# Preparing the linear attention by halves among its chunks, with GpSimd making the differences to the reference columns

## The reference, cut to what matters

```python
cum = jnp.cumsum(gi, axis=2)
diff = cum[:, :, :, None, :] - cum[:, :, None, :, :]
decay = jnp.where(causal, jnp.exp(jnp.where(causal, diff, 0.0)), 0.0)
scores = jnp.einsum('bhid,bhijd,bhjd->bhij', qi, decay, ki)
out = (jnp.einsum('bhij,bhjv->bhiv', scores, vi)
       + jnp.einsum('bhid,bhdv->bhiv', qi * jnp.exp(cum), state))
state = (jnp.exp(last[:, :, 0, :, None]) * state
         + jnp.einsum('bhjd,bhjv->bhdv', ki * jnp.exp(last - cum), vi))
```

## Time and profile before

| | us |
|---|---|
| median of 3 runs (lowest to highest) | 3340.0 (3337.72 to 3342.39) |
| the profiled execution, its time | 3340.4 |
| its span in the trace | 3338.8 |
| `gla_stage`, from its first to its last instruction | 330.2 to 569.8 |
| TensorE busy over the whole span | 2937.0 (88%) |
| VectorE busy over the whole span | 1674.2 (50%) |

### The profile page before, as it was taken

One profiled execution on the slowest core, in us unless ns is written; L12 is line 12 of the kernel. 1 busy time (PEld: TensorE's weight loads), 2 busy tenths in 40 slices (PEclk: granted clock), 3 DMA queues, 4 the chain that ended last, 5 costly groups with the idle time before them and its releaser, 6 DMA issues. The chain is left out here.

```text
span 3338.8 us, 38597 instructions
## 1 busy us (share of the span) xinstructions
PE 2937.0 (88%) x14688; PEld 2323.1 (70%) x14688; DVE 1674.2 (50%) x2776; ACT 979.9 (29%) x1870; POOL 706.7 (21%) x445
## 2 busy tenths in 40 slices
PE   6999456878999999969999799988899998999988
PEld 4767346336888888857768687766677676877766
DVE  4170876223323313232478763476534787634865
ACT  3151221111001001020268342175103673421751
POOL 1233000002333333214111301402141113014021
PEclk8999678888999999989999899999999998999989
DMA  3011001101111121113112001203231120012032
GB/s 106 33 32 38 0 1 50 55 6 67 35 58 51 35 67 45 35 66 105 27 38 76 26 1 51 70 8 126 89 107 26 43 75 23 1 52 73 4 126 89
DMA packets 78797, 168.35 MB, mean 50 GB/s; under 512 B 14848, under 2 KB 33808, under 8 KB 78096
## 3 DMA queue, kind: packets, MB, share of 16 engines
q1 hardware_dynamic: 70160, 140.61, 12.6%
q10 hardware_dynamic: 8448, 25.18, 2.7%
HBM read 128.00 MB, written 20.97 MB: 45 GB/s over the span
## 5 line engine op out<-in xcount | busy, mean ns | idle before, releaser
L296 PE MATMUL psum<-H,ffn_W 128*128 128x512 f32 x672 | 262.8, 391 | 12.8 <-POOL ffn_W L1278 11.1
L297 PE MATMUL psum<-H,ffn_W 128*128 128x512 f32 x672 | 262.3, 390 | 0.0
L298 PE MATMUL psum<-H,ffn_W 128*128 128x512 f32 x672 | 262.2, 390 | 0.0
L1276 POOL CAST ffn_W<-ffn_W 128x1024 fp32r<-128x1024 f32 (+1 forms) x84 | 69.4, 826 | 680.8 <-PE psum L298 447.2
L290 PE MATMUL psum<-CONST 128*128 128x512 f32 x116 | 74.4, 799 | 134.2 <-ACT XT_mixer L1017 77.5
L1573 DVE TENSOR_SCALAR_CACHE_REDUCE MB<-OM,tk_mid 128x512 bf16<-128x512 f32 (+2 forms) x192 | 184.3, 1010 | 2.3
L1352 DVE TENSOR_SCALAR ffn_Y<-ffn_G,ffn_par 128x1024 f32<-128x1024 f32 x21 | 22.1, 1052 | 297.5 <-ACT ffn_G L1341 297.5
L1542 ACT ACTIVATE MB<-OM,tk_mid 128x384 bf16<-128x384 f32 (+2 forms) x192 | 157.0, 819 | 48.5 <-DVE tk_mid L1570 44.4
L482 POOL TENSOR_TENSOR tk_W<-tk_W 128x1024 fp32r<-128x1024 f32 (+1 forms) x38 | 78.7, 2074 | 424.7 <-ACT tk_W L434 424.7
L1278 POOL TENSOR_TENSOR ffn_W<-ffn_W 128x1024 fp32r<-128x1024 f32 (+1 forms) x84 | 161.7, 1925 | 6.7
L296 PEld LDWEIGHTS psum<-H,ffn_W 128*128 128x128 f32 x672 | 126.7, 188 | 40.3 <-POOL ffn_W L1278 11.5
(11 more groups left out here) (417 smaller groups left out, 7502.8 us busy)
## 6 DMA issues: line engine op xcount, KB each, us to landing
OM<-in_w_feat SPq DMA_DIRECT2D x34, 512.0 KB, 4.3
tk_W<-in_w_feat SPq DMA_DIRECT2D x22, 512.0 KB, 3.5
ffn_W<-in_ffn_w_gate SPq DMA_DIRECT2D x21, 512.0 KB, 3.4
ffn_W<-in_ffn_w_val SPq DMA_DIRECT2D x21, 512.0 KB, 3.5
ffn_W<-in_ffn_w_down SPq DMA_DIRECT2D x42, 256.0 KB, 2.7
OM<-MB ACTq DMA_DIRECT2D x64, 128.0 KB, 2.6
OM<-OM ACTq DMA_DIRECT2D x64, 128.0 KB, 3.0
fin_W<-in_w_out SPq DMA_DIRECT2D x4, 2048.0 KB, 10.6
```

Source lines behind the costliest of these rows:

```text
L296: pe.matmul(out, a1, b1, start=start, stop=False)
L297: pe.matmul(out, a1, b2, start=False, stop=False)
L298: return pe.matmul(out, a2, b1, start=False, stop=stop)
L1276: pool.tensor_copy(w1, w).then_inc(rounded, 1)
```

## The change

The preparation is cut into six **units**, the two halves (512 tokens, four chunks) of each of the three tiles, and each unit into three **parts**. Unit 0 is prepared ahead of pass 0. The parts of the others run one by one behind a chunk: unit 1 behind chunks 0 to 2 of pass 0, unit 2 behind its chunks 4 to 6, units 3 and 4 likewise in pass 1, unit 5 behind chunks 0 to 2 of pass 2 (`prep_at`). Pass 3 prepares nothing. Part 0 has the scan and levels 0 and 1, part 1 levels 2 and 3 and `QK`, part 2 levels 4 to 6, `QE` and `KL`. The eight differences of a unit are made by GpSimd (`refer`, a subtraction of 128 by 512), which waits only for the scan (`cums`) and for the four buffers of `Z`, now 512 columns each. `QW` holds each head in its own rows, with no zeros, so the clearing is gone; in return TensorE makes each level's scores as two products, one per head, over 64 rows (32 in passes 2 and 3) and 64 moving columns. The transposes of the keys are made by halves (`keys`), `spin` runs once with four products, and the integer masks are the constant tables read as integers. `place` does the same eight copies as before with another addressing; what it was, and the removed blocks that are printed above, are left out here.

```diff
--- before.py
+++ after.py
@@ -866,19 +866,41 @@
...
+    CH = NT // 2
+    TAIL = 5
+    N_Z = NL + 1
...
     tile_of = [0, 1, 2, 2]
+    pass_of = [0, 1, 2]
     flat = X.rearrange("p t n -> p (t n)")
+    rows_in = [[slice(first + h * dk, first + (h + 1) * dk) for h in range(2)] for first, dk in PASS_ROWS]
+    def prep_at(p, c):
+        if c < 3:
+            return (2 * tile_of[p] + 1, c) if p == 0 or tile_of[p - 1] != tile_of[p] else None
+        if CH <= c < CH + 3:
+            return (2 * tile_of[p + 1], c - CH) if p + 1 < NP and tile_of[p + 1] != tile_of[p] else None
+        return None
+    def freed(u):
+        p, half = pass_of[u // 2], u % 2
+        return NT * (p - 1) + CH * (half + 1) if p else 0
+    def levels_of(part):
+        return ((0, 1), (2, 3), (4, 5, 6))[part]
     with ExitStack() as mem:
         KW = XT[:, 0:NL, :]
         C = XT[:, NL, :]
-        QW = flat[:, 0:NL * S].rearrange("p (n c h m) -> p n c h m", n=NL, c=NT, h=2)
-        QK = flat[:, NL * S:]
-        Z = spare
+        QW = flat[:, 0:NL * HALF].rearrange("p (n c m) -> p n c m", n=NL, c=NT)
+        QK = flat[:, NL * HALF:NL * HALF + S]
+        Z = spare.rearrange("p a n -> p (a n)").rearrange("p (z n) -> p z n", z=4)
         QE = sbuf(nc, mem, "gla_QE", [P, S])
         KL = sbuf(nc, mem, "gla_KL", [P, S])
         EL = sbuf(nc, mem, "gla_EL", [P, NT])
@@ -886,114 +908,119 @@
         SC = sbuf(nc, mem, "gla_SC", [P, 2, 2, 2, P])
         ST = sbuf(nc, mem, "gla_ST", [P, 2, P])
-        LM = sbuf(nc, mem, "gla_LM", [P, NL * 64], INT32)
-        DM = sbuf(nc, mem, "gla_DM", [P, P], INT32)
+        LM, DM = level.bitcast(INT32), ident.bitcast(INT32)
+        def half_of(ap, u):
+            return ap[:, u % 2 * HALF:(u % 2 + 1) * HALF]
         with nc.Block() as block:
             @block.gpsimd
             def _(pool):
-
                 pool.memset(keep, 1.0).then_inc(kept, 1)
                 pool.wait_ge(kept, 1)
                 pool.memset(keep.rearrange("p (c n) -> p c n", n=P)[:, :, 0:1], 0.0).then_inc(kept, 1)
-                for n, p in enumerate((0, 2, 3)):
...
+                def refer(u, seq):
+                    b = P if seq == TAIL else LEVELS[seq if seq < TAIL else seq - 1]
+                    w = b if seq == TAIL else 2 * b
+                    z = Z[:, seq % 4, :].rearrange("p (m w) -> p m w", w=w)
+                    c3 = half_of(C, u).rearrange("p (m w) -> p m w", w=w)
+                    ref = c3[:, :, b - 1:b].to_broadcast([P, HALF // w, w])
+                    if N_Z * u + seq >= 4:
+                        pool.wait_ge(weights, N_Z * u + seq - 3)
+                    if seq == TAIL:
+                        pool.tensor_tensor(z, ref, c3, ALU.subtract).then_inc(refs, 1)
+                    else:
+                        pool.tensor_tensor(z, c3, ref, ALU.subtract).then_inc(refs, 1)
+                for u in range(2 * len(pass_of)):
+                    pool.wait_ge(cums, u + 1)
+                    for seq in range(N_Z):
+                        refer(u, seq)
             @block.vector
             def _(dve):
                 own = Own(dve, own_d)
-                own(dve.tensor_copy(LM[:, :], level))
-                own(dve.tensor_copy(DM[:, :], ident))
                 own(dve.memset(SC, 0.0))
+                own(dve.memset(ST, 0.0))
                 own.wait()
                 dve.wait_ge(kept, 2)
-                for p, (first, dk) in enumerate(PASS_ROWS):
...
+                def weigh(u, n):
+                    g, b = u // 2, LEVELS[n]
+                    dve.wait_ge(weights, N_Z * u + (n if n < TAIL else n + 1) + 1)
+                    w4 = half_of(KW[:, n, :], u).rearrange("p (c m w) -> p c m w", c=CH, w=2 * b)
+                    q4 = half_of(Q[:, g, :], u).rearrange("p (c m w) -> p c m w", c=CH, w=2 * b)
+                    own(dve.tensor_tensor(QW[:, n, CH * (u % 2):CH * (u % 2 + 1), :]
+                                          .rearrange("p c (m w) -> p c m w", w=b),
+                                          w4[:, :, :, b:2 * b], q4[:, :, :, b:2 * b], ALU.mult))
+                    w3 = half_of(KW[:, n, :], u).rearrange("p (m w) -> p m w", w=2 * b)[:, :, 0:b]
+                    k3 = half_of(K[:, g, :], u).rearrange("p (m w) -> p m w", w=2 * b)[:, :, 0:b]
+                    own(dve.tensor_tensor(w3, w3, k3, ALU.mult))
+                def prep(u, part):
+                    g = u // 2
+                    if part == 0:
+                        if freed(u):
+                            dve.wait_ge(out_done, freed(u))
+                        own.then(dve.tensor_tensor_scan(half_of(C, u), half_of(keep, u), half_of(LF[:, g, :], u), 0.0,
+                                                        ALU.mult, ALU.add))
                         dve.sem_inc(cums, 1)
-
...
+                    for n in levels_of(part):
+                        weigh(u, n)
+                    if part == 1:
+                        own(dve.tensor_tensor(half_of(QK, u), half_of(Q[:, g, :], u), half_of(K[:, g, :], u), ALU.mult))
+                    elif part == 2:
+                        own(dve.tensor_tensor(half_of(QE, u), half_of(QE, u), half_of(Q[:, g, :], u), ALU.mult))
+                        own(dve.tensor_tensor(half_of(KL, u), half_of(KL, u), half_of(K[:, g, :], u), ALU.mult))
                         own.wait()
                         dve.sem_inc(mixed, 1)
-                    own.then(dve.memset(ST, 0.0))
+                def place(step):
+                    dve.wait_ge(scored, step + 1)
+                    if step >= 2:
+                        dve.wait_ge(out_done, step - 1)
+                    bank = kit.pair(step % 2).rearrange("p (h n) -> p h n", h=2)
...
+                    own.wait()
+                    dve.sem_inc(placed, 1)
+                for part in range(3):
+                    prep(0, part)
+                for p in range(NP):
+                    rows = rows_in[p]
+                    if p:
+                        dve.wait_ge(out_done, NT * p - 1)
+                        own.then(dve.memset(ST[:, 0, :], 0.0))
                     dve.sem_inc(state_set, 1)
                     for c in range(NT):
                         step = NT * p + c
-                        dve.wait_ge(scored, step + 1)
...
+                        place(step)
                         if c < NT - 1:
-                            if c >= 1:
-
+                            if step:
                                 dve.wait_ge(out_done, step)
+                            if p >= 2 and c == 0:
+                                own.then(dve.memset(ST[:, 1, :], 0.0))
+                            dve.wait_ge(upd_done, step + 1)
...
@@ -1001,33 +1028,50 @@
                                     kit.psum[r, 7, v], ALU.mult, ALU.add)
                             last.then_inc(upd_taken, 1)
                             dve.wait_ge(upd_taken, (NT - 1) * p + c + 1)
+                        if prep_at(p, c):
+                            prep(*prep_at(p, c))
             @block.scalar
             def _(act):
-                own = Own(act, own_a)
+                def bend(u, seq):
+                    act.wait_ge(refs, N_Z * u + seq + 1)
+                    if seq == TAIL:
+                        act.activation(half_of(QE, u), half_of(C, u), ACT.Exp)
...
+                        act.activation(half_of(KL, u), Z[:, seq % 4, :], ACT.Exp).then_inc(weights, 1)
+                        return
+                    n = seq if seq < TAIL else seq - 1
+                    b = LEVELS[n]
+                    z = Z[:, seq % 4, :].rearrange("p (m w) -> p m w", w=2 * b)
+                    w = half_of(KW[:, n, :], u).rearrange("p (m w) -> p m w", w=2 * b)
+                    act.activation(w[:, :, b:2 * b], z[:, :, b:2 * b], ACT.Exp)
+                    act.activation(w[:, :, 0:b], z[:, :, 0:b], ACT.Exp, scale=-1.0).then_inc(weights, 1)
+                def prep(u, part):
+                    if part == 0:
+                        act.wait_ge(cums, u + 1)
+                    for seq in ((0, 1, 2), (3, 4, TAIL), (6, 7))[part]:
+                        bend(u, seq)
+                def keys_turned(u):
+                    act.wait_ge(kt_done, u + 1)
+                    act.activation(half_of(KLT, u), kit.psum[:, 4 + u % 2, :], ACT.Copy).then_inc(kt_taken, 1)
+                for part in range(3):
+                    prep(0, part)
+                keys_turned(0)
                 for p in range(NP):
-                    g = tile_of[p]
...
                     for c in range(NT):
-                        act.wait_ge(out_done, NT * p + c + 1)
+                        step = NT * p + c
+                        act.wait_ge(out_done, step + 1)
                         act.activation(O[:, c, P * p:P * (p + 1)], kit.psum[:, 6, 0:P], ACT.Copy
                                        ).then_inc(out_taken, 1)
+                        if prep_at(p, c):
+                            prep(*prep_at(p, c))
```

(52 more changed lines are left out.)

127 lines of the change are left out of this document (24 added, 103 removed).

## The result

The kernel after takes 3358.6 us (3357.9 to 3360.51, 4 runs), the kernel before 3339.9 (3337.72 to 3342.39, 4 runs): ratio 1.0052, 95% interval 1.004 to 1.0065. It is slower by 18.7 us; forecast were 3326.0 and a range up to 3346.

What follows compares the result with a forecast made beforehand. TensorE's loads bound the steps, VectorE with its ScalarE round trip the preparations, one after the other. Start gains 16.9 us, middle loses 2.5: -14.4 on 3340.4 gives 3326.0 us; range 3303 to 3346.

Steps and rivals of the forecast that it cites:

- TensorE's step: Chunk steps without preparation: scores as 32 load-matmul pairs instead of 16, loads overlapping, 0.25 us more, 3.93 us a step.
- The units: Five units prepared among the chunks, each with the chunk behind it: 28.8 to 33.0 us, 30.9 in the middle.
- The start: Ahead of pass 0: only unit 0 prepared, first chunk placed at 353.4 instead of 370.26, gain 16.9 us.
- The lock: In preparation, GpSimd's differences and VectorE's two-SBUF-tensor operations wait for each other's whole instruction: 1.36 us for one of each.
- The rival that the turns don't bite: In preparation parts, VectorE is held less by GpSimd: at most 21.5 us less, 3304; half of it, 3315; chance 0.24.
- the turns: In the units, VectorE's scan and products alternate with GpSimd's differences, costing about 4 us a unit.
- shared bandwidth: Other reading of VectorE and GpSimd contention: no exclusive lock, so the stalls in the units would be gone.
- the second rival: In the scores, the 16 more loads come one by one at 0.11 us: +33 us, 3359; chance 0.12.
- slow on short runs: GpSimd's differences on references repeated over few columns take 2.4 us each instead of 1.28: +42 us, 3368; chance 0.07.
- Nothing gained: Units of 33 to 34 us, all cold, eat the gain at the start: 3334 to 3345; chance 0.07.

Runs made afterwards that it cites:

- the third throw-away version: Kernel after with the differences back on VectorE and one throw-away product of 128 rows by 128x512 in every step: 3389.6 us, ratio 1.0146 to the kernel before.

## Why the prediction was wrong

**The step that failed** is "A plain step is 3.93 us (3.7 to 4.2)", in "TensorE's step". It took the clock of the earlier trace rows along into products of another form. At that clock it was about right: the first step is 3.76 us. But the half-row products don't keep the clock, and eleven plain steps take 72.2 us (513.08 to 585.32) instead of 11 x 3.93 = 43.2: 29.0 us of the miss. The range had no case in which the clock stays at 0.50 outside the units. That it was the form of the products, and neither a missing spin nor the preparation among the chunks, is shown by three runs: with full-row scores the steps are 3.48 us at 1.00, with a spin they are 6.58 again from the third step on, and in the kernel before half-row scores alone make them 6.56.

**The units** were to take 30.9 us (28.8 to 33.0) and take 30.04 and four times 33.1 to 33.4, in sum 162.9 instead of 154.5: 8.4 us of the miss. 29.0 + 8.4 = 37.4 is all that the loop (235.2) has over the forecast (154.5 + 43.2 = 197.7); less 3.3 at the start and some 2 behind the loop it is the miss of 32.1 us (3358.1 less 3326.0). Half clock had been priced behind a unit and in parts 1 and 2, but it also holds part 0: there VectorE idles 5.05 us before its first product (389.50), since ScalarE's bends stand behind the output copy of 388.58, which a TensorE at half clock brings late. Part 0 is 13.3 us (380.18 to 393.50) instead of 11.3; with full-row scores it is 10.2 and the idle time 2.03 (384.82 there); parts 1 and 2 (7.3 and 7.95) and the chunk behind (4.6) came within 0.5 us of what was priced. With full-row scores the units take 28.3 to 30.8 us.

**The start** was right in kind and a little better: first placing at 350.14 instead of 353.4.

**The lock** held: products of 0.42 us take 1.25 beside GpSimd, alternating with its 1.22, a turn each 1.2 us (389.85, 391.03) where 1.36 was worked out (1.35 by its own terms: 1.28 less 0.23, and 0.425 less 0.13). The rival that the turns don't bite is false. The forecast put the turns at about 4 us a unit, 20 in all; the runs give only the net price of having the differences on GpSimd, 15.6 us of loop. Where the prediction says that with shared bandwidth the sum would be that of the second rival, it means the first, the turns that don't bite. GpSimd is not slow on short runs: four differences, repeated over 128 down to 16 columns, take 4.14 us (384.59), 1.04 each, below the 1.28 that I took; one over 4 columns takes 1.03 (389.76 with full-row scores), and those over 2, each beside a product of VectorE, at most 1.28 (398.61).

**Loads overlap**, so the second rival is false, although its 3359 us came out almost to the digit: 28 loads take 1.64 us. It had named the wrong mechanism, and only the rows tell the two apart; in the total they look the same. The Trainium skill, in "TensorE: Matmul & The Clock Gate", section "LDWEIGHTS (loading the stationary operand)", has a load's time go by its columns; the trace agrees for loads to the same rows (28 in 6.09 us at half clock), but loads that go to different rows in turn overlap (28 in 3.06), so their sum doesn't follow from the time of one.

**"Nothing gained"** said units of 33 to 34 us, all cold, and these came; it too left the plain steps at full clock.

With full-row score products and all else as it is (the separation of the heads left out), the time is 3307 us, inside the range, with the turns as forecast and plain steps of 3.48 us. What stays open is why the form decides: four forms were run and one came to 1.00, which gives no rule, and the third throw-away version shows that the clock can go either way with the code unchanged. The Trainium skill, in "TensorE: Matmul & The Clock Gate", section "Part 1: The HAM clock gate (the "warmup" mystery)", sets the clock by how busy TensorE has been, at 2.4 GHz when busy. By that the last stretch of the kernel after would have run at 1.00; the trace differs (0.50 with TensorE busy for all of 76.52 us), and the measurement decides. Whether busy in the profile's sense is what sets the clock, no run here shows.

## What to carry to other kernels

When a change gives TensorE's products another form (fewer rows, shorter moving operands, more of them), price them at both clock levels and keep both in the range, even where TensorE will never idle: busy time alone doesn't tell the clock granted. Before halving a product to save zeros, count what the zeros cost elsewhere; here they were 28 short VectorE products in pass 3 and seven more a unit, 27.2 us of loop (202.1 less 174.9) against 44.7 for the half-row form. And where TensorE waits anyway for a stage that other engines prepare, throw-away products in that wait may pay for what follows (15.6 us of loop here).

## What the runs showed of the hardware

- TensorE was busy for 76.52 of 76.52 us at a granted clock of 0.50 (1.2 GHz), with 28 of 44 matmuls over 32 rows and 64 columns. With 14 over 128 rows and 128 columns in their place it was 1.00 (2.4 GHz), busy 23.37 of 24.00.
- The clock fell behind a spin that had raised it (1.00 at 546 to 550 us, then 0.66, then 0.50) while TensorE was busy for 11.92 of 12.00 us.
- Throw-away work in idle time raised the clock for the work behind it (0.50 to 1.00, scores 3.19 to 1.73 us); one such product a step in a busy stretch mostly didn't (8.27 us a step instead of 6.57), and did for stretches of 8 to 16 us in two traces (1.00 and 0.97).
- Weight loads to two different row groups overlap at both clocks: 28 in 1.64 us and in 3.06.
- GpSimd's subtraction of a repeated reference column, 128x512, takes 1.04 us alone and 1.22 to 1.28 beside VectorE's products, which take 1.25 there instead of 0.42.
